# A hybrid retention / differential-attention layer on one core: a GpSimd wait moved behind ten additions, and a rotation no longer split around two halves of a running sum

## The reference, cut to what matters

```python
shift1, scale1, gate1, shift2, scale2, gate2 = split(silu(c) @ w_ada + b_ada, 6)   # for c and c_ctx
h = rmsnorm(x, norm1_g) * (1.0 + scale1) + shift1
q_r, k_r, v_r, g_r, q_d, k_d, v_d, gates = split(h @ w_in)
gate_r, gate_d = split(sigmoid(gates + b_gate))
q_r, k_r = rope(q_r), rope(k_r)                     # latent tokens only; first half and second half swapped
y_r = head_group_norm(retention_fwd + retention_bwd)
branch_r = (silu(g_r) * y_r) @ w_ret_out
o_d = rmsnorm(diff_attention(rope(q_d), rope(k_d), v_d)) * (1.0 - lam_init)
branch_d = o_d @ w_diff_out
x = x + gate1 * ((gate_r * branch_r + gate_d * branch_d) @ w_o)
h2 = rmsnorm(x, norm2_g) * (1.0 + scale2) + shift2
x = x + gate2 * ((silu(h2 @ w_ffn_gate) * (h2 @ w_ffn_up)) @ w_ffn_down)
```

## Time and profile before

| | |
|---|---|
| median of 3 runs | 1286.25 us |
| the profiled execution | 1286.38 us, span 1284.7 us |
| PE busy | 1246.8 us, 97% |
| DVE busy | 871.6 us, 68% |
| ACT busy | 513.4 us, 40% |
| POOL busy | 377.6 us, 29% |
| chain that ended last | PE 82%, DVE 7%, POOL 6%, ACT 2% |
| mean granted clock of PE | 0.998 |

### The profile page before, as it was taken

How to read it: one execution, slowest core, us unless ns; L and a number is a source line. 1 busy time by engine, 2 the same in 40 slices (tenths; PEclk the granted TensorE clock), 3 DMA queues, 4 the chain that set the end, 5 groups by cost and what they waited for, 6 DMA issues and landing times.

```text
span 1284.7 us, 19524 instructions
## 1 busy us (share of the span) xinstructions
PE 1246.8 (97%) x7638; PEld 1138.6 (89%) x7638; DVE 871.6 (68%) x1389; ACT 513.4 (40%) x877; POOL 377.6 (29%) x291
## 2 busy tenths in 40 slices
PE   4999999999999999999999999999999999999997
PEld 2698888899999999988788898899998999889986
DVE  3656853477466896375899754489974799558966
ACT  5442222463223443224777522264431344314434
POOL 1012110310655531111899300015500445006400
PEclk9999999999999999999999999999999999999999
DMA  9644542133222435441200125211232123222222
GB/s 309 215 132 139 186 159 82 43 114 119 78 67 83 118 104 168 120 143 56 82 1 2 72 77 187 92 33 44 89 113 85 59 74 99 99 66 66 91 91 82
DMA packets 88054, 129.64 MB, mean 101 GB/s; under 512 B 3545, under 2 KB 64466, under 8 KB 87714
## 3 DMA queue, kind: packets, MB, share of 16 engines
q1 hardware_dynamic: 77024, 95.69, 23.3%
q0 software_dynamic: 8336, 29.58, 7.3%
q10 hardware_dynamic: 2610, 3.20, 1.0%
HBM read 117.43 MB, written 4.73 MB: 95 GB/s over the span
## 4 chain that ended last, share of the span: by engine, by line
PE 82%; DVE 7%; POOL 6%; ACT 2%; issue 1%; DMA 1%; SPq 0%; ACTq 0%; DVEq 0%
PE psum L500 28%; PE psum L461 23%; PE psum L738 22%; POOL probs L1103 3%; POOL probs L1109 3%; DVE seven_lo L768 2%; PE psum L1144 1%; PE psum L447 1%; DMA ada_a<-in_w_ada 1%; PE psum L656 1%; DVE w_lo L425 1%; PE psum L1252 1%; PE psum L1237 1%; PE psum L1250 1%; PE psum L1251 1%
## 5 line engine op out<-in xcount | busy, mean ns | idle before, releaser
L425 DVE TENSOR_TENSOR w_lo<-w_raw,w_hi 128x2048 fp32r<-128x2048 f32 x49 | 115.8, 2364 | 121.9 <-ACT w_hi L420 118.6
L758 ACT ACTIVATE seven_hi<-w_raw 128x512 fp32r<-128x512 f32 x140 | 86.8, 628 | 133.5 <-PE psum L738 85.6
L768 DVE TENSOR_TENSOR seven_lo<-w_raw,seven_hi 128x512 fp32r<-128x512 f32 x140 | 123.7, 914 | 20.8 <-ACT seven_hi L758 20.6
L500 PE MATMUL psum<-w_hi,hid 128*128 128x512 f32 x440 | 135.6, 390 | 0.0
L420 ACT ACTIVATE w_hi<-w_raw 128x2048 fp32r<-128x2048 f32 x49 | 93.6, 1910 | 104.0 <-PE psum L500 64.1
L738 PE MATMUL psum<-h_hi,seven_lo 128*128 128x320 f32 x416 | 128.8, 310 | 1.1 <-DVE silu_g L2247 1.1
L738 PE MATMUL psum<-h_lo,seven_hi 128*128 128x320 f32 x416 | 128.7, 309 | 0.0
L738 PE MATMUL psum<-h_hi,seven_hi 128*128 128x320 f32 x416 | 128.7, 309 | 0.0
L500 PEld LDWEIGHTS psum<-w_hi,hid 128*128 128x128 f32 x440 | 82.7, 188 | 17.1
L461 PE MATMUL psum<-h_hi,w_lo 128*128 128x320 f32 x416 | 96.2, 313 | 0.3 <-DVE w_lo L425 0.3
L500 PE MATMUL psum<-w_lo,h_hi 128*128 128x512 f32 x240 | 94.7, 395 | 1.1 <-ACT mod L1577 1.1
(11 more groups left out here) (357 smaller groups left out, 3185.6 us busy)
## 6 DMA issues: line engine op xcount, KB each, us to landing
w_raw<-in_w_in SPq DMA_DIRECT2D x32, 1024.0 KB, 5.5
w_raw<-in_w_ffn_gate SPq DMA_DIRECT2D x11, 1024.0 KB, 5.3
w_raw<-in_w_ffn_up SPq DMA_DIRECT2D x11, 1024.0 KB, 5.3
ada_b_k<-in_w_ada POOLq DMA_DIRECT2D x18, 512.0 KB, 4.2
ada_a<-in_w_ada SPq DMA_DIRECT2D x8, 1024.0 KB, 13.6
w_raw<-in_w_ffn_down SPq DMA_DIRECT2D x8, 1024.0 KB, 5.1
ada_b<-in_w_ada POOLq DMA_DIRECT2D x14, 512.0 KB, 4.1
w_raw<-in_w_ret_out SPq DMA_DIRECT2D x4, 1024.0 KB, 5.1
```

What stands on the lines that cost most here:

```text
L425: dve.tensor_tensor(w_lo[s][:, :, :], w_raw[s][:, :, :], w_hi[s][:, :, :].bitcast(F32), ALU.subtract).then_inc(w_lo_done, 1)
L500: last = pe.matmul(bank(WIDE_BANKS[i][t]), x[:, k, ts], wide(w, kk), start=(k == 0 and n == 0), stop=(k == kt - 1 and n == 2))
L758: done = act.activation(seven_hi[:, p, :, :], of_weights(p, name, i, par), ACT.Copy)
L768: done = dve.tensor_tensor(seven_lo[:, p, :, :], of_weights(p, name, i, par), seven_hi[:, p, :, :].bitcast(F32), ALU.subtract)
```

## The change

There are two edits, and they are independent of each other.

```diff
@@ gpsimd
             with pool.Fori(0, 2) as i:
                 for par in range(2):
                     load_ada("gate_r", i, par)
-            pool.wait_ge(ada_step, 16 * 13)
             add_token_terms(0, len(terms))
 
             for n, unit in enumerate(gated_units):
                 if n == 1:
+                    pool.wait_ge(ada_step, 16 * 13)
                     pool.dma_start(rope_d[:, :, :], a["const_rope_diff"].rearrange("a p t -> p a t")).then_inc(ld_rope, 16)
                 weight_sums(*unit)
                 last_weight_sum(*unit)
@@ vector
             rotate_first(0, 1)
             dve_split(dve, 4, 0)
             rotate_first(1, 0)
-            ada_partial("v_r", 0, 0, range(KT // 2))
-            rotate_first(1, 1, lambda: ada_partial("v_r", 0, 0, range(KT // 2, KT)))
+            rotate_first(1, 1)
+            ada_partial("v_r", 0, 0)
             dense_wide("v_r", nothing)
             dense_wide("g_r", nothing)
```

## The result

| | before | after |
|---|---|---|
| median | 1286.26 us (4 runs) | 1318.18 us (4 runs, 1317.7 to 1319.56) |
| ratio | | 1.0251, 95% interval 1.0233 to 1.0269 |
| span of the profiled execution | 1284.7 us | 1316.1 us |
| PE busy | 1246.8 us, 97% | 1252.3 us, 95% |
| POOL busy | 377.6 us | 373.9 us |

What follows compares the result with a forecast made beforehand. TensorE (PE), busy 97% of the span, was taken to bound the kernel. PE stalls of 6.1 and 22.6 us plus 2.8 us of lower clock made 31.5 on 1286.38 us: 1317.7, stated as 1317.5 us, range 1308 to 1323.

Steps and rivals of the forecast that it cites:

- Edit 1, first the order, then POOL's company: v_r sums behind the rotation: they and the split end late, POOL's operations add turns; PE stalls 6.1 us (3.4 to 6.8).
- The rotation gains nothing: At the v_r sums: the rotation starts and ends at the same times, since its waits were for ScalarE and the DMA.
- Edit 2, the turns: gate_r sums: freed h_sum operations alternate with DVE's small ones, 3.25 us per turn; PE waits 22.6 us (20 to 24).
- The clock: PE after both waits: lower clock adds 2.2 us (0 to 2.8) at gate_r, 0.6 (0 to 2.8) at v_r.
- The reading by the Trainium skill: PE's clock: idling causes the lower level, so the short v_r wait pays in full too, 2 us above the sum.
- The reading behind the 2.8 us: Run's first L1144, after PE idled: 16 took 6.36 us, the next 16 took 3.62; 2.74 lost at the lower clock.
- The sum: Whole kernel: 6.1 + 22.6 + 2.8 = 31.5 us on 1286.38 us, so 1317.7, stated as 1317.5 us.
- Rival 1: gate_r sums: small DVE operations slip past POOL's, only v_r costs; 1293 us; chance 0.11 together with rival 4.
- rival 4: h_sum operations: something else holds POOL until about 331, so freeing them does nothing; 1293 us; 0.11 together with Rival 1.
- rival 3: PE's later places: later waits absorb the shift, so not slower; 1286 us; chance 0.03.
- Rival 2: Both places: lower clock in full after both waits, v_r at its upper bound; 6.8 + 24 + 5.5, 1322.7 us; chance 0.06.

Runs made afterwards that it cites:

- edit 1 alone: Kernel before with only the v_r modulation sums changed, all 16 now behind the rotation: 1294.64 us (ratio 1.0064).
- `e4_pool_quiet`: Kernel before with all 16 v_r sums behind the rotation, and POOL's two L1003 and two copies held until the second unit's split is done: 1291.69 us (1.0040).
- `e6_four_early`: Kernel before with four of the ten h_sum operations let ahead of POOL's wait: 1292.97 us (1.0056).
- the full edit: Kernel before with only POOL's wait changed, so all ten h_sum operations start early: 1308.98 us (1.0180).
- `e9_sums_pe_fed`: Kernel before with all 16 v_r sums behind the rotation, and PE's wait for them filled with 21 idle matmuls: 1292.75 us (1.0055).
- `e7_quarters`: Kernel before with all ten h_sum operations freed from POOL's wait, each cut into four of 128x320: 1296.12 us (1.0088).
- `e3_second_half_late`: Kernel before with only the second half of the v_r sums moved behind the rotation: 1291.80 us (1.0041).

## Why the prediction was right

The cause, both places and the order of size were right. The sum was closer than its terms: 1317.5 against 1318.18 us is in part luck, as two errors of 2 us cancelled.

- *Edit 1, first the order, then POOL's company.* Forecast 6.1 us until the second unit starts, measured 6.5. The split ended 9.1 us later than in the trace before, corrected for the start (127.52 + 0.78 against 119.2); forecast 128.0 - 119.2 = 8.8. (The working's own terms give 122.6 + 2.9 = 125.5 and 127.7, 0.3 less than it wrote.) POOL's four operations cost 2.95 us by experiment (edit 1 alone less `e4_pool_quiet`). Nothing behind it was late, as forecast.
- *The rotation gains nothing.* Right: it still ended on the swap's landing.
- *Edit 2, the turns.* POOL's start (forecast 319.9, measured 328.19 - 8.4 = 319.8), the end of the split, and one small operation for each POOL operation were right. The mis-sized term is the turn: I stretched it to 3.25 us by what a longer DVE operation had cost POOL, but here an operation of 256 columns cost POOL nothing, and the turn is 3.02. Seven turns make 1.6 us of the 2.0 by which the wait of 22.6 was too long; it is 20.6. `e6_four_early` and the full edit give 2.63 us for each POOL operation from the fifth on.
- *L1928.* It was left open whether it is held, as it would move the end by under 1 us. It is: 6.10 us for two.
- *The clock.* The term most out of size is "for the 6.1 us wait it is open: +0.6": the clock fell there in full, 2.6 us, and 2.4 (0.9 + 1.5) at the second place where I had 2.2. Together 5.0 against 2.8. The reading by the Trainium skill that stood beside my sum ("TensorE: Matmul & The Clock Gate", idle time as the cause, 2 us above the sum) was the better one for the first place, and `e9_sums_pe_fed` shows the cause.
- *Where the price of the clock came from.* The reading behind the 2.8 us was weaker than it looks. In the trace before, the mean of 0.998 comes from the last 6 us (granted clock 0.50 from 1279 us on, when PE has nothing left to do), and not from a stretch with matmuls. For the first 16 L1144 the column of the granted clock reads 1.00, but the trace has no record of the clock before 22.5 us, which is about where they end; so it neither shows nor excludes the lower level there. Only their length speaks for it. That the price was of the right size at the second place is shown by the new traces, in which the granted clock does read 0.50.
- *The sum.* 31.5 forecast; 31.3 by the trace's parts (6.5 + 20.6 + 5.0 less 0.8 of a quicker start). The turns were 2.0 us too dear and the clock 2.2 us too cheap.
- *Rivals.* Rival 1 (small operations slip past) is refuted by the trace and by `e7_quarters`; rival 4 (POOL held otherwise) by POOL's start at once behind its last load; rival 3 by PE's waits later on, which are the same as before but for 0.3 us for `w_lo`. Rival 2 had the clock nearly right (5.5 for 5.0) and the turns wrong.

## What to carry to other kernels

Before a GpSimd operation is set free to start earlier, look at what VectorE does then: each of its operations with two SBUF inputs waits for one whole GpSimd instruction that reads SBUF, so that a train of n small ones loses up to n times the length of a GpSimd instruction, as long as GpSimd has instructions left, however little work they have. A wait that looks superfluous for the data may stand there for this; if the work must overlap, cut the GpSimd instructions short (20.5 us of wait became 7.4) or let so few of them start early that what VectorE loses stays inside the slack (two early operations held a split by 2.2 us, and PE had 2.9 to spare). And before work is moved out of a gap in which its engine waits for a transfer, read how late the next thing that TensorE needs will be; add the clock to every new TensorE wait.

## What the runs showed of the hardware that I had not expected

- What a DVE operation costs POOL depends on both. In the changed kernel, 128x1280 operations of POOL kept their step of 3.02 us with a 128x256 operation of DVE between each two, while a 128x2048 one stretched POOL's next to 4.9. POOL's shorter ones did lose: pieces of 128x320 took 1.0 us each instead of 0.84 (`e7_quarters`), two copies of 128x256 1.14 us instead of 0.73.
- The lower clock came with waits of 2.2 and 2.4 us, and not with the 1.15 us of `e9_sums_pe_fed`. In `e3_second_half_late` it came while PE still stood: PE's last full matmul ended at 120.9, the granted clock was 0.95 over 122.5 to 123.0 and 0.50 from there, and the L447 began at 123.24. In `e4_pool_quiet` it came 0.6 us after the first L447 had begun. In the changed kernel it fell 2.7 us after PE's last matmul at the first place and some 5.3 us after it at the second. It cost 2.0 to 3.4 us at a time (the slower L447 of the second place included), about as much after the short waits (2.0 and 2.4) as after the one of 20.5 us (2.4).
- While the clock was low, the eight L447 took 1.87 us against 0.95.
